# Two modulation chunks moved from VectorE, GpSimd and ScalarE to TensorE

## What is computed

```
def ada_params(cond, w_mod, b_mod):
    m = jax.nn.silu(cond) @ w_mod + b_mod
    ...
mx = ada_params(c, w_mod[i], b_mod[i])
x = x + 0.5 * mx[2] * swiglu(modulate(rms_norm(x, norm_g[i, 0]), mx[0], mx[1]),
                             ffn1_w_gu[i], ffn1_w_d[i])
...
my = ada_params(c_ctx, w_mod[i], b_mod[i])
y = y + 0.5 * my[2] * swiglu(modulate(rms_norm(y, norm_g[i, 0]), my[0], my[1]), ...)
```

## Time and profile before

| | us |
|---|---|
| median of three runs | 3697.46 |
| lowest and highest | 3697.26, 3703.94 |
| the profiled execution | 3697.62 |
| its span | 3695.4 |
| PE busy in the span | 3490.1 (94%) |
| PE's first instruction | 61.97 |
| first matmul of the feed-forward stage | 75.84 |

### The profile page before, as it was taken

One profiled execution on the slowest core, in us unless ns is written; L12 is line 12 of the kernel. 1 busy time (PEld: TensorE's weight loads), 2 busy tenths in 40 slices (PEclk: granted clock), 3 DMA queues, 4 the chain that ended last, 5 costly groups with the idle time before them and its releaser, 6 DMA issues.

```text
span 3695.4 us, 40300 instructions
## 1 busy us (share of the span) xinstructions
PE 3490.1 (94%) x16978; PEld 2876.7 (78%) x16978; DVE 1934.6 (52%) x2662; ACT 1252.0 (34%) x1778; POOL 361.2 (10%) x204
## 2 busy tenths in 40 slices
PE   2999999899979999999999999989999998999998
PEld 2888888787868888788877888766788876678887
DVE  8434343566655453645344333486564648666464
ACT  4322122344433222322233222324442432445242
POOL 3311001111100000000000000320100033010001
PEclk9999999899999999999999999989999999999998
DMA  5423242010115353535222222210232212013221
GB/s 195 142 80 127 86 141 71 34 35 35 35 57 171 126 195 124 182 127 181 91 74 87 96 98 91 89 64 6 69 103 97 97 66 90 6 52 103 97 97 57
DMA packets 95797, 348.81 MB, mean 94 GB/s; under 512 B 10624, under 2 KB 11136, under 8 KB 95104
## 3 DMA queue, kind: packets, MB, share of 16 engines
q1 hardware_dynamic: 94320, 343.06, 27.6%
q10 hardware_dynamic: 1296, 3.18, 0.2%
HBM read 344.10 MB, written 2.10 MB: 94 GB/s over the span
## 4 chain that ended last, share of the span: by engine, by line
PE 84%; DVE 10%; ACT 4%; issue 1%; POOL 1%; DMA 0%; ACTq 0%; DVEq 0%; POOLq 0%
PE PS L343 83%; DVE CAC L1949 2%; ACT G L1160 1%; DVE ST L1755 1%; PE PS L419 1%; DVE WL L1517 1%; DVE X L1928 1%; DVE PTL L1738 1%; DVE G L1619 0%; ACT WH L971 0%; DVE HL L1627 0%; POOL SM L2243 0%; ACT PTH L1141 0%; DVE X L1925 0%; DVE HL L1933 0%
## 5 line engine op out<-in xcount | busy, mean ns | idle before, releaser
L343 PE MATMUL PS<-HH,WH 128*128 128x512 f32 (+1 forms) x3120 | 1193.6, 383 | 38.0 <-DVE HL L1627 16.9
L343 PE MATMUL PS<-HL,WH 128*128 128x512 f32 (+1 forms) x3120 | 1177.8, 378 | 0.0
L343 PE MATMUL PS<-HH,WL 128*128 128x512 f32 (+1 forms) x3120 | 1173.8, 376 | 0.0
L1517 DVE TENSOR_TENSOR WL<-RAW,WH 128x1024 fp32r<-128x1024 f32 x462 | 584.5, 1271 | 766.9 <-ACT WH L971 766.8
L971 ACT ACTIVATE WH<-RAW 128x1024 fp32r<-128x1024 f32 x496 | 522.4, 1057 | 1140.6 <-PE PS L343 1123.0
L343 PEld LDWEIGHTS PS<-HH,WH 128*128 128x128 f32 x3120 | 594.9, 191 | 155.4 <-DVE HL L1627 19.1
L343 PEld LDWEIGHTS PS<-HL,WH 128*128 128x128 f32 x3120 | 594.5, 191 | 109.5 <-issue 5.5
L343 PEld LDWEIGHTS PS<-HH,WL 128*128 128x128 f32 x3120 | 593.6, 190 | 108.8
L343 PE MATMUL PS<-AH,WH 128*128 128x512 f32 x1392 | 526.7, 378 | 1.7 <-DVE WL L1517 1.7
L343 PE MATMUL PS<-AL,WH 128*128 128x512 f32 x1392 | 524.1, 377 | 0.0
L343 PE MATMUL PS<-AH,WL 128*128 128x512 f32 x1392 | 522.9, 376 | 0.0
(11 more groups left out here) (275 smaller groups left out, 3253.9 us busy)
## 6 DMA issues: line engine op xcount, KB each, us to landing
RAW<-wst SPq DMA_DIRECT2D x640, 512.0 KB, 3.3
X<-xT SPq DMA_DIRECT2D x1, 2048.0 KB, 12.2
out<-X SPq DMA_DIRECT2D x8, 256.0 KB, 2.0
PTF<-cb SPq DMA_DIRECT2D x1, 1024.0 KB, 4.7
Y<-yT SPq DMA_DIRECT2D x1, 1024.0 KB, 7.6
PTF<-cb ACTq DMA_DIRECT2D x1, 1024.0 KB, 4.8
HM<-sg ACTq DMA_DIRECT2D x4, 256.0 KB, 3.7
ROPE<-rope SPq DMA_DIRECT2D x1, 512.0 KB, 4.6
```

The source lines that it names most:

```text
L343: return e.matmul(o, l, r, start=start, stop=stop)
L1517: e.tensor_tensor(lo, raw_block(s), f32(hi), ALU.subtract).then_inc(*did("dve_done", ("wlo", b)))
```

## The change

The sixteen blocks of chunks 0 and 1 are laid with inputs on partitions. They go into a region of their own, `FM` (64 KB of each partition, over the space of HH, HL and AH, which nothing uses yet), so SP issues them without a wait, each with its own semaphore. A small array `CC` (128 x 16) holds c and c_ctx as columns. TensorE makes chunks 0 and 1 as 16 x 8 matmuls of a 128 x 128 piece of FM against two columns of CC, in plain float32, behind the spread of the norm and ahead of the first feed-forward matmul. DVE adds the biases from PSUM. In SP's order x and y now come first. The order `stream` is shorter ahead of the norm: on ACT and DVE block 16 is split behind the root and the reciprocal, block 17 in the middle of the norm, and the modulation blocks 18 and 19, which stood ahead of the norm, come behind it, as does ACT's silu of CB.

```diff
+    FM = at("FM", OHH, 16384)
...
-        todo = [(l, j) for l in range(2) for j in range(72)]
+        todo = [(l, j) for l in range(2) for j in range(72) if l or j >= 16]
...
+        def first_modulation():
+            o, _ = hold("mod0", 32, 6, ("modb", 0, 1))
+            q.wait_ge("columns")
+            for j in range(16):
+                descs.extend([(("w_mod", 0, k * 128, j * 128, 128, 128, 0),) for k in range(8)])
+                q.wait_ge("raw", j)
+                for k in range(8):
+                    m = mm(o[:, 2 * j:2 * j + 2], first_block(j)[:, k * 128:(k + 1) * 128], CC[:, 2 * k:2 * k + 2], k == 0, k == 7)
+            m.then_inc(*did("pe_done", ("tile", "mod0")))
...
-        modulation(16)
-        upto["start"] = 17 + NHL - 1
         squares("f00")
-        ffn("f00", norm("f00"))
+        xs = norm("f00")
+        first_modulation()
+        upto["start"] = 18
+        ffn("f00", xs)
```

On ScalarE, in the norm and in the main sequence:

```diff
+            if st == "f00":
+                part(upto[LAST[st]], 1)
             q.wait_ge("mod", l, 3 * i)
...
-                if k >= 2:
+                if k == 3 if st == "f00" else k >= 2:
                     part(upto[LAST[st]], 1)
...
+        q.wait_ge("columns in")
+        e.activation(CC[:, :], CC[:, :], ACT.Silu).then_inc(*did("act_done", ("columns",)))
+        for m in range(8):
+            square("in", m)
+        prepare(ACT.Sqrt, "sqrt", "f00")
+        stream(16)
+        norm("f00")
         q.wait_ge("cond in")
         e.activation(CB, CB, ACT.Silu).then_inc(*did("act_done", ("cond",)))
-        for m in range(8):
-            stream(2 * m + 2)
-            if m >= 3:
-                square("in", m - 3)
-        for m in range(5, 8):
-            square("in", m)
-        prepare(ACT.Sqrt, "sqrt", "f00")
-        stream(upto["start"])
-        norm("f00")
         ffn("f00")
```

On VectorE, the new step and its place in the norm:

```diff
+        def first_modulation():
+            m0, m1 = MOD[:, 0:16], MOD[:, 16:32]
...
+            q.wait_ge("tile", "mod0")
+            e.tensor_tensor(m1, bank["mod0"][:, 16:32], v1("bm", 16, 16), ALU.add).then_inc(*did("dve_done", ("modb1",)))
+            e.tensor_tensor(m0, bank["mod0"][:, 0:16], v1("bm", 0, 16), ALU.add).then_inc(*did("dve_done", ("modb", 0, 1), ("mod", 0, 0)))
+            q.wait_ge("modb1")
+            e.scalar_tensor_tensor(out=m1, in0=m1, scalar=1.0, in1=v1("ng", 0, 16), op0=ALU.add, op1=ALU.mult).then_inc(*did("dve_done", ("mod", 0, 1)))
...
+            if st == "f00":
+                part(upto[LAST[st]], 1)
+                first_modulation()
             q.wait_ge("tile", ("sp", st))
...
-                if k >= 3:
+                if k == 4 if st == "f00" else k >= 3:
                     part(upto[LAST[st]], 1)
```

On SyncE:

```diff
+        e.dma_start(CC[:, :], cc).then_inc(*did("columns_in", ("columns in",), by=16))
+        e.dma_start(Xt[:, :], xT).then_inc(*did("x_in", *[("x", "in", m) for m in range(8)], by=16))
+        e.dma_start(Yt[:, :], yT).then_inc(*did("y_in", *[("y", "in", m) for m in range(8)], by=16))
...
+            for j in range(2, 14):
+                first(j)
+            weights(16)
...
+        for d in range(16 + NRAW, nblk):
```

More of the change, by code:

```diff
@@ L131, in wait_ge, with program @@
             self.eng.wait_ge(self.sems[sem], value)
-def program(nc, wst, vec1, vec2, cst, rope, rope96, xT, yT, sg, cb, out, order, old):
+def program(nc, wst, vec1, vec2, cst, rope, rope96, xT, yT, sg, cb, cc, out, order, old):
     ctx = ExitStack()
@@ L971, in stream @@
                     e.activation(split_block(b)[0], raw_block(s), ACT.Copy).then_inc(*did("act_done", ("whi", b)))
-                else:
+                elif order[s][0] == 0 and order[s][1] < 40:
                     l, j = order[s]
[L974 to L979, removed]
+                    q.wait_ge("gprod", l, j)
+                    q.wait_ge("mod zero")
+                    e.activation(PROD, PROD, ACT.Copy, accum_out=mcol(l, j // 8, j % 8, 1)).then_inc(*did("act_done", ("gacc", l, j)))
             pos = max(pos, to)
@@ L1517, in stream @@
                         e.tensor_tensor(lo, raw_block(s), f32(hi), ALU.subtract).then_inc(*did("dve_done", ("wlo", b)))
-                else:
+                elif order[s][0] != "P":
                     modulation(s, *order[s])
@@ L1535, in modulation @@
                 q.wait_ge("cond2")
[L1536 to L1548, removed]
+            if l == 0 and ch < 5:
+                q.wait_ge("gprod", l, j)
+            e.tensor_tensor_reduce(raw, raw, CB[:, 0:1024], 1.0, 0.0, ALU.mult, ALU.add, mcol(l, ch, k, 0)).then_inc(*did("dve_done", ("gx", l, j)))
             if k == 7:
@@ L2180, in _ @@
         e.memset(MOD[:, :], 0.0).then_inc(*did("dve_done", ("mod zero",)))
[L2181 to L2185, removed]
+        for m in range(1, 7):
             square_sum(m)
-        stream(upto["start"])
         lam()
+        stream(16)
         norm("f00")
@@ L2225, in stream @@
                         e.tensor_tensor(lo, raw_block(s), f32(hi), ALU.subtract).then_inc(*did("pool_done", ("wlo", b)))
-                else:
+                elif order[s][0] == 0 and order[s][1] < 40:
                     l, j = order[s]
[L2228 to L2236, removed]
+                    q.wait_ge("raw", s)
+                    q.wait_ge("cond")
+                    if product_read:
+                        q.wait_ge("gacc", *product_read)
+                    product_read = l, j
+                    e.tensor_tensor(PROD, raw_block(s), CB[:, 1024:2048], ALU.mult).then_inc(*did("pool_done", ("gprod", l, j)))
             pos = max(pos, to)
@@ L2383, in _ @@
         q = Queue(e, sems, table)
-        e.dma_start(CB, cb).then_inc(*did("cond_in", ("cond in",), by=16))
[L2385 to L2405, removed]
@@ new lines, in _ @@
+        if nblk:
+            first(0)
+            first(1)
+        e.dma_start(VA[:, :], vec1[:, 0:V1["lam"][0]]).then_inc(*did("consts_in", by=16))
+        e.dma_start(CST[:, :], cst).then_inc(*did("consts_in", ("consts",), by=16))
+        e.dma_start(LAMV[:, :], vec1[:, V1["lam"][0]:NV1]).then_inc(*did("lam_in", ("lam in",), by=16))
+        if nblk:
+            for j in range(2, 14):
+                first(j)
+            weights(16)
+            first(14)
+            first(15)
+            weights(17)
@@ new lines, in _ @@
+        e.dma_start(CB, cb).then_inc(*did("cond_in", ("cond in",), by=16))
+        if nblk:
+            weights(18)
+            weights(19)
+        e.dma_start(ROPE[:, :], rope).then_inc(*did("rope_in", ("rope in",), by=16))
+        for d in range(16 + NRAW, nblk):
+            prev = d - NRAW
+            if order[prev] is None:
+                q.wait_ge("wlo", halves[prev])
+            else:
+                l, j = order[prev]
+                q.wait_ge("gx", l, j)
+                if l == 0 and j < 40:
+                    q.wait_ge("gprod", l, j)
+            weights(d)
@@ L2470, in make @@
                 dt("rope", (128, 1024)), dt("rope96", (128, 1024)), dt("xT", (128, 4096)), dt("yT", (128, 2048)),
-                dt("sg", (2, 128, 1280)), dt("cb", (128, 2048)), dt("out", (128, 4096), "ExternalOutput"))
+                dt("sg", (2, 128, 1280)), dt("cb", (128, 2048)), dt("cc", (128, 16)), dt("out", (128, 4096), "ExternalOutput"))
         return nc, *program(nc, *args, order, old)
     descs = make([], None)[1]
-    order = [tuple(d[1:]) if d and d[0] == "T" else None for d in descs[::UPB]]
+    order = [tuple(d[1:]) if d and d[0] == "T" else ("P", n) if d and d[0][0] == "w_mod" else None for n, d in enumerate(descs[::UPB])]
     nblk = len(order)
```

26 lines of the change are left out of this document (17 added, 9 removed).

## The result

The changed kernel took 3719.77 us, the median of four runs (3716.71 to 3725.17), beside 3697.36 for the kernel before on the same chip. The ratio is 1.0062, with a 95% interval of 1.0047 to 1.0077. The forecast was 3716, range 3706 to 3723. A repetition on another chip gave 3722.03 beside 3702.41, ratio 1.0058 [1.0042, 1.0074]; one of the seven executions of the kernel before there ran in a slower state (5027 us) and doesn't count in that ratio. So the change makes the kernel slower by some 0.6%, or 20 to 22 us.

What follows compares the result with a forecast made beforehand. TensorE bounds the kernel, at nine tenths or more almost everywhere except the first slice. A stage start 9.1 us later plus u1 another 9.0 later gives 3697.6 + 18.1 = 3715.7, so 3716, range 3706 to 3723.

Steps and rivals of the forecast that it cites:

- 256 passes: TensorE's modulation: 128 float32 matmuls of two passes each, at 0.2125 us a pass, 54.4 us in all.
- S: Start of the feed-forward stage, its first matmul: 84.9 us, 9.1 later than the 75.84 before.
- stop ahead of g1: Behind the norm, TensorE waits some 9 us before feed-forward product g1, while ACT handles moved blocks 18 and 19.
- u1: Feed-forward product released by the silu of g0 on ACT; starts at S + 41.5 instead of S + 32.5, 9.0 later.
- The clock: TensorE's modulation row: low level (granted clock 0.50) taken for all 256 passes, 54.4 us against 26.6 at the high level.
- The transfers: Sixteen modulation blocks at 420 GB/s: last lands at 32 us, TensorE reads it at 77.4, so they stay hidden.
- The order on ACT: Behind the norm, silu of CB and blocks 18 and 19 precede block 20's split, so g1 waits until 27 to 28 after S.
- the path to the modulation: Kernel start, from x and y through the norm's sums and spread: TensorE is free for the modulation at 26.4 us.
- the bullet on blocks 22 to 27: Chain behind the norm: block 22 done at 28.2 after S, 23 at 31.9, 26 at 36.9, 27 at 40.6; u1 at 41.5.
- the clock rises and stays up: Rival for the modulation: passes cost 0.104 us, S is 58.8 and the time 3690, near the bound of faster; 12%.
- the stop is hidden: Rival behind the norm: ACT's chain is shorter than added up, only the later S counts, 3707; 5%.
- each block costs more: Rival in the modulation: semaphore waits empty TensorE's queue sixteen times, or a pass is 0.219 and more, 3722; 8%.

Runs made afterwards that it cites:

- burst: Kernel after, plus sixteen 512-column fp32r matmuls, results unread, in a row ahead of block 5 of the modulation; 3722.85 us beside 3702.41 for the kernel before.
- half: Kernel after, leaving out every second of the eight 128-row pieces of each modulation block on TensorE; 3695.65 us, ratio 0.9982.
- ahead20: Kernel after, with silu of CB and modulation blocks 18 and 19 put back ahead of the norm; 3710.42 us, ratio 1.0026.
- burst_keep: As burst, plus one 512-column matmul behind every two narrow ones from block 5 on; 3742.09 us beside 3702.41 for the kernel before.
- wide8: Kernel after, plus one plain float32 matmul of 512 columns, result unread, behind every eight narrow ones of the modulation; 3749.42 us, ratio 1.0128.

## Why the prediction was right, step by step

| step | predicted | measured |
|---|---|---|
| x and y read by ACT | 8.4, 10.9 | 9.02, 11.51 |
| sums of squares ready | 18.0 | 19.1 |
| TensorE free for the modulation | 26.4 | 27.8 |
| 256 passes | 54.4 | 54.6 |
| first G | 81.4 | 82.97 |
| S | 84.9 (+9.1) | 86.66 (+10.8) |
| stop ahead of g1 | some 9 | 9.20 |
| u1 | S + 41.5 (+9.0) | S + 44.7 (+12.2) |
| given back behind u1 | 0 | 1.4 |
| sum, against the span | +18.1 | +21.6 |
| the same against the profiled time | +18.1 | +21.2 |

**The clock** was the choice on which the forecast rested, and it held: 0.2133 for every pass, 54.6 us in all. It was taken from a stretch of 3.4 us and carried to one of 54, against the rule of "TensorE: Matmul & The Clock Gate", Part 1 in the Trainium skill. That rule says that sustained matmul activity releases the throttle. With it the trace doesn't agree: TensorE was busy for 54.6 us without a break, and the last passes cost what the first did. `burst` shows the fall of the clock under such a row. In part the choice was lucky: in four of the eleven profiled executions with this row the clock stood at 1.00 for 3.4 us near its start, which is worth 3.1, and the prediction knew only the two ends, all high or all low.

**The transfers** cost nothing between the blocks, as argued; `half` shows it at twice the speed of reading. They cost 0.6 us ahead of x, which I had by a rate alone.

**The order on ACT** was right in its mechanism. `ahead20` shows it: without it no stop ahead of g1, and u1 13.5 us earlier.

**What was mis-sized** are two terms. The first is the path to the modulation: 1.4 us too short. The transfers of x and y give 0.6 of it. The six sums on DVE give another 0.6: one takes 0.96, but in a row they begin 1.06 apart, so that the six took 6.27 and not 5.7. The rest is in the hand-overs, 0.1 of it in the adding (23.9 and 2.6 are 26.5). With 0.2 for the passes and 0.1 behind them, S is 1.7 later than added up. The second is the bullet on blocks 22 to 27, 3.2 us too short. Three rows of the kernel after show why:

```profile
114.91 3.13 POOL L2248 TENSOR_TENSOR PTF<-RAW,PTF 128x1024 f32<-128x1024 f32 x1 [1.32 <-DMA RAW<-wst]
115.73 3.38 DVE L1554 CUSTOM_DVE_ANT_0 RAW<-RAW,PTF 128x1024 f32<-128x1024 f32 x1
...
123.30 2.38 POOL L2248 TENSOR_TENSOR PTF<-RAW,PTF 128x1024 f32<-128x1024 f32 x1 [5.26 <-DMA RAW<-wst]
```

DVE's sum of block 22 began at 115.73 and took 3.38 beside POOL's product of block 23, so the buffer that block 26 needs came free late, and POOL waited 5.26 us for that transfer. The prediction had named the pair of DVE and POOL as a reason for a wider range, but priced the chain with both at their short durations. Block 26 was reckoned to land near 33.5 after S; its product starts at 36.6.

The two misses are 1.7 and 3.2, together 4.9, and 1.4 came back behind u1, for which the prediction had nothing; part of it is the shorter time at the low clock there. So the sum was 3.5 short of the span, and 3716 was 3.8 below the median.

**The rivals.** That the clock rises and stays up is refuted by the passes. That the stop is hidden is refuted by the 9.20. That each block costs more is refuted by `half` and by 54.6 for all. That 3722 comes near the measured time is no support for it: the excess lies elsewhere.

## What to carry to other kernels

A long row of narrow matmuls like this one (plain float32, two columns) is to be priced at the low clock, however busy the engine looks: take the price from a narrow row in the trace that stands alone, not from one inside dense work. When work is moved off an engine, look at what stood behind it in the order of the others, since the gap that it leaves ahead of a norm was a cover for the blocks next in line; here that cost more than the slower start. And an engine that helps another through a shared way to memory may take more than it gives: try it without the help.

## What the runs showed of the hardware

- The granted clock fell from 1.00 to 0.50 while TensorE was busy without a break in narrow matmuls (plain float32, two columns): at 53.5 in `burst` and at 31.8 in `burst_keep`. With one matmul of 512 columns behind every two narrow ones it still fell (`burst_keep`, 0.50 from 60 to 80 us).
- The same passes at the same place ran at either level at first: 80 of them took 17.07 us in `burst` and 13.97 in `burst_keep`.
- A pass of a float32 matmul with 512 columns took 0.85 to 0.93 us at the low level (`wide8`); the fp32r ones of the same width took 6.26 / 16 = 0.39 (`burst`, in which the level rose on the way, at 50.1).
- The fused product and sum on DVE over 128x1024 took 1.22 us alone and 3.35 to 3.38 beside a product on POOL, ending 1.1 us behind the product (7.59 in the kernel before, 115.73 in the kernel after). Two on DVE alone are cheaper than one beside POOL.
